# A recurrent branch reordered: merge gates in eight PSUM banks first, then the output gates, then the output products alone

## The reference, cut to what matters

```python
xc = causal depthwise conv of width 4 (h @ W_xc) + conv_b      # 1280 channels
r = sigmoid(blockdiag(xc, w_a) + b_a)                           # 16 blocks of 80 x 80
i = sigmoid(blockdiag(xc, w_x) + b_x)
log_a = -8 * r * softplus(-lam); a = exp(log_a)
state[t] = a[t] * state[t-1] + sqrt(max(1 - exp(2 * log_a), 0)) * (i * xc)
y_c = state * silu(h @ W_zc)
merged = sig(ga) * (y_a @ Wa) + sig(gb) * (y_b @ Wb) + sig(gc) * (y_c @ Wc)
x = x + rmsnorm(merged @ w_out)
```

## Time and profile before

| what | value |
|---|---|
| median of 3 runs | 2581.47 us (2581.16 to 2584.94) |
| the profiled execution | 2583.16 us |
| its span, first to last instruction | 2581.3 us |
| TensorE busy | 2324.1 us, 90% |
| VectorE / ScalarE / GpSimd busy | 1145.0 / 942.4 / 1123.6 us |
| mean granted TensorE clock | 0.961 |
| chain that ended last | PE 69%, DVE 20%, ACT 6% |

### The profile page before, as it was taken

How to read it: one execution, slowest core, us unless ns; L and a number is a source line. 1 busy time by engine, 2 the same in 40 slices (tenths; PEclk the granted TensorE clock), 3 DMA queues, 4 the chain that set the end, 5 groups by cost and what they waited for, 6 DMA issues and landing times.

```text
span 2581.3 us, 27556 instructions
## 1 busy us (share of the span) xinstructions
PE 2324.1 (90%) x10074; PEld 1753.1 (68%) x10074; DVE 1145.0 (44%) x1829; ACT 942.4 (37%) x1573; POOL 1123.6 (44%) x1380
## 2 busy tenths in 40 slices
PE   6998787999789978999998999799789999989996
PEld 4685455865467745887886777477458878877774
DVE  5767654337624164142246732351551321467422
ACT  4546542245523442232224622333422322236221
POOL 3552133531145402564465655254024654656551
PEclk8999898999899999999999999899999999999998
DMA  3221022221122202232232223122013322322231
GB/s 126 76 90 38 28 69 71 90 66 34 34 75 84 86 17 66 91 97 90 82 99 81 74 82 106 50 79 84 25 51 96 99 90 83 97 82 74 90 94 45
DMA packets 52405, 193.01 MB, mean 75 GB/s; under 512 B 5936, under 2 KB 6192, under 8 KB 51632
## 3 DMA queue, kind: packets, MB, share of 16 engines
q1 hardware_dynamic: 51120, 186.54, 22.9%
q10 hardware_dynamic: 1152, 4.72, 0.5%
HBM read 189.14 MB, written 2.10 MB: 74 GB/s over the span
## 4 chain that ended last, share of the span: by engine, by line
PE 69%; DVE 20%; ACT 6%; issue 3%; POOL 1%; DMA 1%; DVEq 0%; ACTq 0%; SPq 0%
PE proj L450 18%; PE proj L451 18%; PE proj L452 18%; PE stat L446 3%; PE score L446 3%; DVE tmp L1578 2%; DVE y L1230 2%; DVE h L1230 2%; DVE small L1306 2%; DVE y L1229 2%; PE score L450 2%; PE score L451 1%; PE score L452 1%; PE turned L446 1%; PE ptp L644 1%
## 5 line engine op out<-in xcount | busy, mean ns | idle before, releaser
L402 POOL TENSOR_TENSOR lower<-raw_ring,upper 128x256 fp32r<-128x256 f32 x1376 | 1123.4, 850 | 1404.3 <-ACT upper L887 1404.2
L450 PE MATMUL proj<-h,upper 128*128 128x512 f32 x1568 | 643.6, 410 | 62.8 <-issue 16.4
L452 PE MATMUL proj<-h,lower 128*128 128x512 f32 x1568 | 620.6, 396 | 0.0
L451 PE MATMUL proj<-h,upper 128*128 128x512 f32 x1568 | 620.6, 396 | 0.0
L887 ACT ACTIVATE upper<-raw_ring 128x1024 fp32r<-128x1024 f32 x344 | 358.7, 1056 | 642.1 <-PE proj L450 456.0
L450 PEld LDWEIGHTS proj<-h,upper 128*128 128x128 f32 x1568 | 300.7, 192 | 138.5 <-issue 41.3
L451 PEld LDWEIGHTS proj<-h,upper 128*128 128x128 f32 x1568 | 300.2, 191 | 65.6 <-issue 7.2
L452 PEld LDWEIGHTS proj<-h,lower 128*128 128x128 f32 x1568 | 300.0, 191 | 64.5
L450 PE MATMUL proj<-y,upper 128*128 128x512 f32 x752 | 310.8, 413 | 29.7 <-ACT state L954 17.3
L451 PE MATMUL proj<-y,upper 128*128 128x512 f32 x752 | 300.4, 399 | 0.0
L452 PE MATMUL proj<-y,lower 128*128 128x512 f32 x752 | 300.3, 399 | 0.0
(11 more groups left out here) (250 smaller groups left out, 2937.1 us busy)
## 6 DMA issues: line engine op xcount, KB each, us to landing
raw_ring<-stream SPq DMA_DIRECT2D x344, 512.0 KB, 3.5
x<-x_in SPq DMA_DIRECT2D x4, 512.0 KB, 7.1
rows<-rows_in ACTq DMA_DIRECT2D x2, 1024.0 KB, 5.0
out<-x SPq DMA_DIRECT2D x1, 2048.0 KB, 6.3
memraw<-mem_in SPq DMA_DIRECT2D x1, 1024.0 KB, 11.5
memraw<-mem_in ACTq DMA_DIRECT2D x1, 1024.0 KB, 5.0
rot<-tables_in ACTq DMA_DIRECT2D x1, 512.0 KB, 3.3
ws<-ws_in ACTq DMA_DIRECT2D x2, 256.0 KB, 5.3
```

Of the source, the lines that this page charges most:

```text
L402: ins = nc.gpsimd.tensor_tensor(lower[:, p % RING, a:b], raw_ring[:, p % RAWS, a:b], upper[:, p % RING, a:b].bitcast(FP32), ALU.subtract)
L450: first_ = nc.tensor.matmul(o, lhsT[0], rhs[0], start=start, stop=False)
L451: nc.tensor.matmul(o, lhsT[0], rhs[1], start=False, stop=False)
L452: return first_, nc.tensor.matmul(o, lhsT[1], rhs[0], start=False, stop=stop)
```

## The change

1. The 1280 recurrent channels are permuted on the host (weights only), so that in each half (five tiles, eight blocks of 80) four tiles hold one whole block and 48 channels of another, and the fifth holds four strips of 32. The gate products of a half become 24 matmuls on all 128 rows, two runs of 12 matmuls on 32 rows (four row groups, four banks, one after the other in turn), 24 on 64 rows (two row groups, two banks), and 6 on all rows. That is again 78 matmuls in a half, 156 in a layer; the slots `lg` fall from seven to four.
2. The gate jobs of a half use eight banks and then two again; `i` gets four buffers instead of two (over `sq` and `std`).
3. All eight `c.merge` jobs come right after the gate jobs, each in a bank of its own, and wait there for ScalarE, which does its exponentials and roots first, with three feeds put between them. Then ten `zc` jobs, then eight `c.proj` jobs in a row. The merge gates go to eight buffers of their own.
4. VectorE does all ten scans first, and gates and splits afterwards as the silu gates come. Each `merged` tile is split right after it is made.
5. The rates are done before the convolutions.
6. At the passage to `b`, VectorE does the first inverse of the memory keys after `h` tile 1 and the second after tile 2.

```diff
-GATE_BLOCKS = [(i, o) for o in range(LT) for i in range(LT)
-               if any(max(i * P, b * LB) < min(i * P + P, b * LB + LB)
-                      and max(o * P, b * LB) < min(o * P + P, b * LB + LB) for b in range(LW // LB))]
+def lru_channel(t, p):
+    at, k = 8 * (t // 5), t % 5
+    if k == 4:
+        return (at + 4 + p // 32) * LB + 48 + p % 32
+    if k % 2:
+        return (at + k) * LB + p if p < LB else (at + 4 + k) * LB + p - LB
+    return (at + 4 + k) * LB + p if p < 48 else (at + k) * LB + p - 48
+LRU = np.array([lru_channel(t, p) for t in range(LT) for p in range(P)])
...
-    out += names("xc", LT) + names("lg", 7) + names("zc", LT) + branch_out("c", LT)
+    out += names("xc", LT) + names("lg", 4) + names("c.merge", KT) + names("zc", LT) + names("c.proj", LT)
...
+    ig = place("ig", at_sq, [P, 4, SEQ])
...
+    def lru_bank(j, n):
+        return token_bank(j, n % 8) if n % 8 < 4 else [ptp, mix, turned, stat][n - 4]
+    def c_gate(d):
+        return xpad[:, d // 2, d % 2 * SEQ:d % 2 * SEQ + SEQ] if d < 4 else (gate if d < 6 else std)[:, d % 2, :]
...
-            at = j % 2 if at is None else at
+            at = (j % 2 if n < 2 else n) if at is None else at
+            bank_ = proj[at] if at < 2 else lru_bank(j, n)
...
+            def lru_gates(half):
...
+                t0 = 5 * half
+                for g in range(2):
+                    jobs = []
+                    for k in range(4):
+                        w = block(5 * g + k)
+                        jobs.append(opened(4 * g + k))
+                        if g == 0:
+                            pe.wait_ge(*S.after("xc", t0 + k))
+                        begun, _ = products(jobs[k][1], w, both(y, t0 + k, 0, SEQ), True, False)
+                        if k == 0:
+                            release(W, begun)
+                        plans["released", jobs[k][0]] = W.gone
+                    w = block(5 * g + 4)
+                    if g == 0:
+                        pe.wait_ge(*S.after("xc", t0 + 4))
+                    for term, (u, v) in enumerate(TERMS):
+                        for k, (j, bank_) in enumerate(jobs):
+                            rows_ = slice(32 * k, 32 * k + 32)
+                            ins = mm(bank_, w[u][rows_, :], y[rows_, t0 + 4, v, :], False, term == 2)
+                            if term == 2:
+                                ins.then_inc(*S.mark("projected", ("job", j)))
+                W.finish(f"lg{2 * half}")
+                jobs = [opened(8), opened(9)]
+                def across(pairs, start, stop):
+                    for n, (g, k) in pairs:
+                        w = block(12 + n)
+                        for term, (u, v) in enumerate(TERMS):
+                            for low in range(2):
+                                rows_ = slice(HD * low, HD * low + HD)
+                                j, bank_ = jobs[(g + low) % 2]
+                                last = stop and (n, term) == (pairs[-1][0], 2)
+                                ins = mm(bank_, w[u][rows_, :], y[rows_, t0 + k + low, v, :],
+                                         start and (n, term) == (pairs[0][0], 0), last)
...
+                pairs = list(enumerate(ACROSS))
+                across(pairs[0:2], True, False)
+                for g, (j, bank_) in enumerate(jobs):
+                    products(bank_, block(10 + g), both(y, t0 + 4, 0, SEQ), False, False)
+                pe.wait_ge(*S.after("rows_summed", half))
+                across(pairs[2:4], False, True)
+                W.finish(f"lg{2 * half + 1}")
+            for half in range(2):
+                lru_gates(half)
+            for d in range(KT):
+                s = W.slot(f"c.merge{d}")
+                job(S, C, W, [(f"c.merge{d}", s(k * P, k * P + P), both(h, k, 0, SEQ), None) for k in range(KT)], n=d)
+                W.finish(f"c.merge{d}")
             for t in range(LT):
-                mine = [n for n, (_, o) in enumerate(GATE_BLOCKS) if o == t]
-                for g in range(2):
-                    at = 2 * mine[0] + g * len(mine)
...
-            W.finish("lg6")
-            group(S, C, W, names("zc", 4), h, None)
-            for t in range(4, LT):
                 full(S, C, W, f"zc{t}", h, None)
-            out_and_merge("c", LT)
+            for d in range(KT):
+                pairs = []
+                for k in range(LT):
+                    n = LT * d + k
+                    w = W.slot(f"c.proj{n // 8}")
+                    pairs.append((f"c.proj{n // 8}", w(n % 8 * P, n % 8 * P + P), both(y, k, 0, SEQ),
+                                  ("y", "c", k) if d == 0 else None))
+                job(S, C, W, pairs)
+                W.finish_at(W.at["c.proj0"] + LT * (d + 1) // 8)
+            for at in range(4, 8):
+                pe.wait_ge(*S.after("read", last_at.pop(at)))
...
-            act.wait_ge(*S.after("xpad_zero"))
-            for t in range(LT):
-                take(S, C, xpad[:, t % 2, 3:3 + SEQ], keys_=[("xraw", t)],
-                     waits=[("xraw_used", t - 2)] if t >= 2 else [("u_used", KT - 1)])
             tables()
...
             nc.scalar.activation(lam8[:, 0, :], lam8[:, 0, :], ACT.Ln, bias=1.0).then_inc(*S.mark("rates", ("rate2",)))
+            act.wait_ge(*S.after("xpad_zero"))
+            for t in range(LT):
+                take(S, C, xpad[:, t % 2, 3:3 + SEQ], keys_=[("xraw", t)],
+                     waits=[("xraw_used", t - 2)] if t >= 2 else [("u_used", KT - 1)])
             act.wait_ge(*S.after("rates"))
-            for t in range(LT):
-                take(S, C, state[:, t, :], ACT.Sigmoid, keys_=[("r", t)], bias=lc(l, "b_a", t))
-                take(S, C, sq[:, t % 2, :], ACT.Sigmoid, keys_=[("ig", t)], waits=[("gx", t - 2)] if t >= 2 else [],
-                     bias=lc(l, "b_x", t))
+            act.wait_ge(*S.after("std_used", C.n["norm"] - 1))
+            for half in range(2):
+                t0 = 5 * half
+                for n in range(10):
+                    t = t0 + (n % 4 if n < 8 else 4)
+                    bank_ = lru_bank(C.n["job"], n)
+                    if n in (0, 1, 2, 3, 8):
+                        take(S, C, state[:, t, :], ACT.Sigmoid, keys_=[("r", t)], bias=lc(l, "b_a", t), bank_=bank_)
+                    else:
+                        take(S, C, ig[:, t % 4, :], ACT.Sigmoid, keys_=[("ig", t)],
+                             waits=[("gx", t - 4)] if t >= 4 else [], bias=lc(l, "b_x", t), bank_=bank_)
             tables()
+            ahead = C.n["job"]
             for t in range(LT):
                 act.wait_ge(*S.after("r", t))
                 act.wait_ge(*S.after("gx", t))
                 act.wait_ge(*S.after("a2", t))
                 nc.scalar.activation(state[:, t, :], state[:, t, :], ACT.Exp, scale=lam8[:, 0, t:t + 1])\
                     .then_inc(*S.mark("decay", ("a", t)))
+                if t % 4 == 3:
+                    feed(plans["released", ahead + t // 4 + 1] + RING)
             for t in range(LT):
                 loaded[0] = None
                 act.wait_ge(*S.after("rest", t))
                 nc.scalar.activation(late[:, t, 0, :], late[:, t, 0, :], ACT.Sqrt)\
                     .then_inc(*S.mark("decay", ("mult", t)))
+                if t == 4:
+                    feed(plans["released", ahead + 3] + RING)
+            for d in range(KT):
+                take(S, C, c_gate(d), ACT.Sigmoid, keys_=[("c_gate", d)], bank_=lru_bank(C.n["job"], d))
             for t in range(LT):
-                take_gate(S, C, ACT.Silu, block=t if t < 4 else 0)
-            out_and_merge()
+                take(S, C, sq[:, t % 2, :], ACT.Silu, keys_=[("z_gate", t)], waits=[("z_gate_used", t - 2)] if t >= 2 else [])
+            for d in range(KT):
+                next_job(S, C)
...
-                memory(1)
+                units = memory(1)
+                inv = norm_in(S, C, h, x, lambda k: fc("kv_norm", k), ("kv",), keep=gate[:, 0, :],
+                              aside=lambda k: next(units) if k in (1, 2) else None)
+                for _ in units:
+                    pass
...
-                    if s == "c" and d == KT - 1:
-                        for k in range(KT - 1):
-                            split(S, h[:, k, :, :], merged[:, k, :], ("merged", k))
...
             link(S, nc.vector.memset(xpad[:, :, 0:3], 0.0), ("xpad_zero",))
+            dve.wait_ge(*S.after("rate2"))
+            lam = lcols[:, l, LAYER_COLS["lam"]:LAYER_COLS["lam"] + LT]
...
+            link(S, nc.vector.tensor_scalar(lam8[:, 0, :], lam8[:, 0, :], -8.0, None, ALU.mult), ("rates",))
             for t in range(LT):
                 C.next("job")
                 dve.wait_ge(*S.after("xraw", t))
...
-            dve.wait_ge(*S.after("rate2"))
...
             j0 = C.n["job"]
             C.n["job"] += 2 * LT
             for t in range(LT):
                 dve.wait_ge(*S.after("ig", t))
```

(23 more changed lines are left out.)

93 lines of the change are left out of this document (56 added, 37 removed).

## The result

The changed kernel takes 2503.2 us (median of 4 runs, 2500.12 to 2505.36) against 2583.2 for the kernel before on the same chip: ratio 0.9689, 95% interval 0.9672 to 0.9706, 3.1% faster. The forecast was 2494 with a range of 2484 to 2517: direction and mechanism hold, and the gain is 80 us where 88 were forecast. The profiled execution took 2501.2 us, 82.0 less than the profiled one before, so on equal terms 6 us are missing; the rest is spread between executions.

The account below looks back on a forecast made before the run. TensorE, busy 90% of the span, was taken as the bound, with its waits and slow clock. Both layers' 76.3 us plus 11.9 at the passage to `b` made 88.2, from 2583.2 to a forecast of 2494 us, range 2484 to 2517.

Parts of the forecast that it names:

- the branch: Branch c of a layer, first gate matmul to first `wo` matmul: 183.7 us against 218.0, 34.3 less.
- gain of a layer, `wo0` with it: Branch c plus 3.7 us of wait and lower clock in `wo0`: 38.0 us; both layers 76.3.
- one step of 0.230 us: TensorE in branch c: step per matmul where nothing is waited for, `h` and `y` mixed, from 355 matmuls in 81.7 us.
- The passage: Passage to `b`: ScalarE released at 421.6 instead of 433.45; slot copies, GpSimd's halves and TensorE's start move 11.9 us.
- The strips: Gate products: fours and pairs run together at 0.32 us, a mode change adds 0.09; a half takes 13.3 us against 17.9.
- The low end of 11.0: Gate half with weight loads hidden: 6.9 us of full matmuls plus 18 x 0.23, 11.0 us.
- The first rival: Gates: small matmuls do not run together; 21 us, 2515, or with loads exposed 38 us, 2532. Chance 0.14.
- The stops of the gates: New waits: 1.7 us between the gate halves, 0.8 before `c.merge0`, together 2.5 us a layer.
- The slots last too: Merge jobs under the decay chain: weight slots are fed before TensorE needs them; late next would be `zc0`'s slot.
- The second rival: Decay chain: TensorE starves, a feed late or waiting in ScalarE's queue; some 8 us a layer, 2510. Chance 0.09.
- The waits that the order removes: Branch c: waits of 8.5 (first sigmoid), 5.4 (silu gates), 3.9 (`y`) and 2.0 us (`merged`) go.
- The clock: Rival: lower clock in the gates, +53, 2547; through the reordered branch, 2860. Chance 0.05, 0.02 slower than before.

Follow-up runs that it names:

- passage_old: Changed kernel with only the passage from a to b put back, both memory-key inverses after all eight `h` tiles: 2511.9 us, ratio 0.9722.
- no_feeds: Changed kernel without the three feeds between ScalarE's exponentials and roots: 2523.1 us, ratio 0.9766.
- feed_after: Changed kernel with ScalarE making the silu gate first and feeding the next slot after it in the `zc` jobs: 2500.7 us, ratio 0.9675.
- all_rows: Changed kernel with every strip and half matmul of the gates made over all 128 rows, same number and order: 2522.2 us, ratio 0.9764.
- strips_serial: Changed kernel with the 32-row matmuls ordered by strip, three in a row on the same row group: 2504.9 us, ratio 0.9688.
- merge_late: Changed kernel with gates packed but the rest of branch c in the old order, no feeds in the decay chain, late splits: 2536.3 us, ratio 0.9817.
- rates_late: Changed kernel with the rates after the convolutions again, on ScalarE and VectorE: 2516.5 us, ratio 0.9735.
- split_late: Changed kernel with seven splits of `merged` kept until just before the last product is read: 2516.5 us, ratio 0.9735.
- each alone: Changed kernel with only the second gate half's banks turned by two, 2501.4 us, or only the gate before the feed in `zc` jobs, 2500.7 us.
- both together: Changed kernel with the second gate half's banks turned by two and the feed after the gate in `zc` jobs: 2493.2 us, ratio 0.965.

## Why the prediction held, and where it was off

| step | forecast, us | measured, us |
|---|---|---|
| gates of a layer with their stops | 29.1 | 28.92 |
| merge and `zc` jobs | 99.4 | 99.70, a wait of 1.4 in it |
| output products | 55.2 | 56.23 |
| the branch | 183.7 | 184.9 |
| gain of a layer, `wo0` with it | 38.3 and 38.0 | 37.6 and 37.1 |
| passage to `b`, read at the start of layer 0's branch | 11.9 | 7.2 |
| sum | 88.2 | 81.9 between the spans |

The gain of layer 0 is read from how far the branch's start lies ahead of the earlier trace rows: 7.2 us (1375.50 to 1368.29) in layer 0, 44.8 (2283.70 to 2238.88) in layer 1. Two rows of the table agree better than their terms do: the forecast used one step of 0.230 us, and the windows give 0.2276 over `h` (merge and `zc` jobs, without their wait) and 0.234 over `y` (output products). So the 1.4 us wait hides in the first, and the second is 1 us longer.

**The passage is the step that failed.** The prediction said that the slot copies, GpSimd's halves and TensorE's start would all move by the 11.9 us that ScalarE is released earlier. The start did: ScalarE's root, then TensorE's first matmul of the group, come 12.3 us earlier (421.11 for 433.45; 424.25 for 436.54), of which TensorE was 0.5 us early already before the passage (last memory matmul at 421.37 for 421.87). ScalarE, GpSimd and TensorE at the passage in the changed kernel:

```profile
421.11 0.48 ACT L1009 ACTIVATE half_var<-stat,small 128x256 f32<-128x256 f32 x1 [4.70 <-DVE std L1323]
```

```profile
422.91 7.87 POOL L422 TENSOR_TENSOR lower<-raw_ring,upper 128x256 fp32r<-128x256 f32 x8 [3.77 <-ACT upper L975]
```

```profile
424.25 0.47 PE L470 MATMUL proj<-h,upper 128*128 128x512 f32 x1 [2.60 <-ACT vm L1042]
...
426.83 0.49 PE L470 MATMUL score<-h,upper 128*128 128x512 f32 x1 [0.95 <-POOL lower L422]
...
430.83 0.79 PE L470 MATMUL score<-h,upper 128*128 128x512 f32 x1 [3.04 <-POOL lower L422]
```

and GpSimd in the kernel before, then its TensorE:

```profile
435.25 6.01 POOL L402 TENSOR_TENSOR lower<-raw_ring,upper 128x256 fp32r<-128x256 f32 x8 [15.61 <-ACT upper L887]
```

```profile
436.54 0.76 PE L450 MATMUL proj<-h,upper 128*128 128x512 f32 x1 [14.39 <-DVE km L1225]
...
441.32 0.50 PE L450 MATMUL score<-h,upper 128*128 128x512 f32 x1 [0.61 <-POOL lower L402]
```

GpSimd makes the halves of two slots in 7.9 us instead of 6.0, and the second slot's first use comes only 10.5 us earlier (430.83 for 441.32). In the kernel before, VectorE was all but done when this began; now six of its eight `h` tiles and the second inverse are still to do and run beside it, and both engines' instructions are longer: GpSimd's 0.98 for 0.75 us, and VectorE's inverse operation twice that of 4 us before:

```profile
419.73 0.43 DVE L1321 TENSOR_TENSOR half_var<-half_var,std 128x256 f32<-128x256 f32 x1
...
423.61 0.83 DVE L1321 TENSOR_TENSOR half_var<-half_var,std 128x256 f32<-128x256 f32 x1
```

The Trainium skill ("SBUF — State Buffer", Who interferes with whom) says that a VectorE instruction with two SBUF inputs contends with a GpSimd instruction that reads SBUF, over a shared port pair that is locked exclusively. The longer times on both sides agree in sign. passage_old is the test that they come from running side by side: with VectorE's `h` tiles back in front, the same eight GpSimd instructions take 6.02 us again. That the port pair is the reason is the page's account; no run here separates it from another.

Then the clock. In both kernels TensorE runs at the lower level after one stop of the passage. Before, that stop was the long one at the start, and the 9 slow matmuls behind it ended before GpSimd's next halves were there, so they cost nothing (the wait at 441.32 above is 0.61 us). Now the clock falls in the stop of 3.0 us, and the 14 slow matmuls have nothing left to wait for:

```profile
429.80:436.70 6.90, 5.87 (x14) 4.61 (x15) 6.66 (x8) 1.06 (x1) 5.08 (x5) 0.51 0.27 81
```

From the second slot's first use to the end of the group it was 19.9 us (441.32 to 461.2) and is 22.6 (430.83 to 453.4): 2.7 more, as 14 matmuls at 0.43 instead of 0.23 make 2.8. This term differs between executions: in the traces of no_feeds and feed_after, with the same passage, the stretch at the lower level is half as long (mean clock 0.84 from 429 to 440 us, for 0.69 in the changed kernel), and the passage takes 30.7 us instead of 32.0. So 12.3 less 1.8 less 2.7 leaves 7.8; another 0.6 is lost before the recurrent branch, which I did not follow up. With the old passage back it is 8.6 in medians and 7.4 inside the traces, the same within the spread.

**The strips: right in kind, the price too high.** The rows had pairs of unrounded matmuls only, and 0.11 us at both widths was read as a weight load that is not hidden and put on every pair. The step inside a mode is 0.23: the load is hidden. In the earlier trace rows only the first step after a change of row mode is to be seen, and the changed kernel has the same 0.11 there (0.34 for 0.23) and not at the steps after it: it is part of the price of the change. A change of mode costs 0.21 where 0.09 was put down. The two errors cancel in part: 7 changes at 0.12 more are 0.8 us, 18 steps at 0.09 less are 1.6, together 12.5 for 13.3; 12.7 was measured. That the half came out within 0.6 us of the forecast is in part luck. The low end of 11.0 left out the changes of mode altogether. The gain of packing, 18 us, is confirmed by all_rows (19). The first rival, that small matmuls do not run together, falls. "TensorEngine Tiling (Array Packing)", Key Properties, in the Trainium skill, has a mode change drain the engine. The rows show 0.1 us at each border; the strip starts 0.33 us after a full matmul whose record lasts 0.40, so it does not wait for the end of the record (whose length is modelled, so a drain is neither shown nor excluded). The Trainium skill says in the same section that tiles work in parallel and independently, which strips_serial bears out. The Trainium skill's "TensorE: Matmul & The Clock Gate", Part 3, gives 3.07 times for four row tiles of K=32 at N=512: 12 strips in 0.90 us against 12 x 0.23 is 3.07 here as well, though over three fours and both borders; inside the mode it is four strips a step of 0.23. On loads, a point of the same Part 3 of the Trainium skill says that they overlap with matmuls in flight only where the row group differs; the full-row stream here, a load of 0.19 us before each matmul and a step of 0.23, does not agree.

**The stops of the gates: term too small by 0.7 us a layer.** The prediction had the two jobs at the start of half two as one wait of 1.7; the trace has a stop at each of them, 0.9 and 1.5. The last, 0.8, was right.

**"The slots last too": right under the decay chain, wrong after it.** ScalarE's chain of layer 1:

```profile
2270.27 1.28 ACT L964 ACT_TABLE_LOAD   x1
...
2285.23 1.06 ACT L975 ACTIVATE upper<-raw_ring 128x1024 fp32r<-128x1024 f32 x1 [0.69 <-DMA raw_ring<-stream]
...
2297.93 1.09 ACT L1042 ACTIVATE xpad<-proj 128x512 f32<-128x512 f32 x2
```

The last gate product starts at 2266.6 and the first merge gate at 2297.9: 31 us, as worked out. No merge job waits, and the feed behind the eighth pair stands only 0.69 us for its transfer. But when the chain is over the stream has to make up, and the transfers set the pace: the prediction named a slot of `zc0` as late next, and it was a feed in `zc2`'s way, 1.4 us. The second rival's mechanism (a feed that blocks ScalarE's queue) is thus real, at 1.4 us a layer where the rival had 8; without the three feeds it would have been 8.0.

**The waits that the order removes: right.** 8.5, 5.4, 3.9 and 2.0 us are gone. They come back when their part is undone: `y` 3.9 and the silu gates 3.2 in merge_late, 4.3 for the rates, 3.9 for the splits, which stand alone now and so are not the 8.5 and 2.0 of the earlier trace rows. These reversals cost more than their waits, since the clock falls with them: rates_late 2 x 4.3 us of waits, and 13 us in time. The forecast took the clock only into `wo0` by name; the rest of it was in the 0.230 step that it used for all. **The clock** rival falls: 1.00 in the strips too.

## What to carry to other kernels

A start that moves forward is a gain only as far as the next engines in line can follow: before the whole shift is booked, look at what will run beside the work that was moved (here VectorE beside GpSimd) and at where the next stop will leave the clock. A price read from the first step after a change holds for that step alone. Banks and feeds have to be moved together: each alone gave 2 or 3 us, both together 10. A copy that may wait for a transfer belongs behind the instruction that somebody waits for, not ahead of it.

## What the runs showed of the hardware that I had not expected

- Row groups of TensorE do not wait for each other's place in the program: strips written one group after the other start in fours 0.01 to 0.02 us apart.
- Inside a mode, the weight loads of partial rows are hidden (a step of 0.23 us at 512 columns, rounded); a change of row mode costs 0.21 us, half at the border and half at the next step.
- GpSimd's subtraction of 128x256 took 0.75 us with VectorE mostly idle (the kernel before and passage_old) and 0.98 beside a busy VectorE, whose 0.43 us operation went to 0.83.
- Whether the granted clock falls after a stop is not given by the longest stop alone: one of 2.1 us was followed by 3.4 us at the lower level, two of 1.0 us with the second 2 us behind the first (split_late) by 6.8 us, and the three of 0.8 to 1.5 us in the gates by none; at the passage the 9 matmuls behind a stop of 2.6 us still ran at full speed. What decides between them is left open.
